# Loading FFN up-projection weights into the input projection's buffer during the prompt mixer

## The reference

```python
h = rmsnorm(x, g_mix) * (1.0 + scale_m) + shift_m
proj = h @ w_in                                   # 1024 -> 3072
q, k, v, g_ret, x_lru, g_lru = jnp.split(proj, offs, axis=-1)
o, s_ret_new = retention(rotary(q), rotary(k) * d ** -0.5, v, s_ret)
ret_out = silu(g_ret) * groupnorm(o)
xc, s_conv_lru_new = causal_dwconv(x_lru, s_conv_lru, conv_lru_w, conv_lru_b)
hl, s_h_new = rg_lru(xc, s_h, pos, w_r, b_r, w_i, b_i, lam)
lru_out = hl * gelu(g_lru)
x = x + gate_m * (jnp.concatenate([ret_out, lru_out], axis=-1) @ w_out)

h = rmsnorm(x, g_ffn) * (1.0 + scale_f) + shift_f
u = h @ w_up_conv                                 # 1024 -> 2816
gv = h @ w_up_gate                                # 1024 -> 2816
uc, s_conv_ffn_new = causal_dwconv(u, s_conv_ffn, conv_ffn_w, conv_ffn_b)
x = x + gate_f * ((gelu(uc) * gv) @ w_down)       # 2816 -> 1024
y = rmsnorm(x, g_final)
```

## Time and profile before

| | us |
|---|---|
| two timed runs | 1499.32 and 1509.76, median 1504.54 |
| the profiled execution | 1513.84 |
| its span on the slowest core, core 4 | 1512.2 |
| spans of the eight cores | 1488.4 to 1512.2 |
| mean granted TensorE clock of the cores | 0.822 to 0.835 of full speed |
| busy on core 4: PE, DVE, ACT, POOL | 985.5, 732.6, 416.2, 199.4 |

### The profile page before, as it was taken

The page is one execution under the profiler, slowest core; times in us unless marked ns, Lnnn a source line. Parts: engine busy times, 40 slices in busy tenths (PEclk is TensorE's granted clock), DMA queues, the critical chain, the costliest instruction groups (busy, mean ns, idle before and its releaser), DMA issues.

```text
span 1512.2 us, 15593 instructions; the slowest of 8 cores (1488.4 to 1512.2 us)
## 1 busy us (share of the span) xinstructions
PE 985.5 (65%) x4378; PEld 462.6 (31%) x4453; DVE 732.6 (48%) x1699; ACT 416.2 (28%) x702; POOL 199.4 (13%) x238
## 2 busy tenths in 40 slices
PE   1115517176677766777551799789878986998554
PEld 0002414133333333333221344334333333433222
DVE  0012045156677777777721364267426742674253
ACT  1000020235533424413302333233223323331011
POOL 1001000121211321311221200100010001000200
PEclk9557556588888999988785799899989998899877
DMA  9957523310101211100138993310031003000220
GB/s 154 173 92 115 112 71 102 125 42 15 42 1 42 84 42 42 57 28 28 57 119 173 180 171 61 124 43 1 1 125 43 1 0 126 15 1 26 87 43 8
DMA packets 46526, 104.85 MB, mean 69 GB/s; under 512 B 3428, under 2 KB 15169, under 8 KB 46393
## 3 DMA queue, kind: packets, MB, share of 16 engines
q0 software_dynamic: 18016, 38.54, 16.2%
q1 hardware_dynamic: 28041, 64.95, 13.5%
q10 hardware_dynamic: 384, 0.36, 0.1%
HBM read 120.29 MB, written 22.09 MB: 94 GB/s over the span
## 4 chain that ended last, share of the span: by engine, by line
PE 38%; DVE 20%; DMA 14%; issue 11%; ACT 8%; POOL 4%; another core or an unknown queue 3%; SPq 1%; DVEq 1%; POOLq 0%; ACTq 0%; PEldq 0%
PE ps L163 35%; DMA sb_wada<-w_ada 4%; DMA sb_wug_sb<-w_upg 3%; PE ps L166 3%; DVE sb_acc L187 3%; DMA sb_xa<-x_scr 3%; DVE sb_xc L187 2%; DVE sb_mq L179 2%; ACT sb_acc L176 1%; SPq L198 1%; DVE sb_ig L187 1%; DVE sb_xc L662 1%; DVE sb_hT L184 1%; DVE sb_yo L187 1%
## 5 line engine op out<-in xcount | busy, mean ns | idle before, releaser
L163 PE MATMUL ps<-sb_h2T,sb_wuc_sb 128*128 128x512 bf16 x688 | 173.0, 393 | 15.4 <-ACT sb_h2T L176 6.4
L163 PE MATMUL ps<-sb_wdn_sb,sb_aT 128*128 128x512 bf16 x692 | 166.0, 403 | 16.9 <-DVE sb_aT L179 14.2
L163 PE MATMUL ps<-sb_h2T,sb_wug_sb 128*128 128x512 bf16 x688 | 168.7, 385 | 3.0 <-DMA sb_wug_sb<-w_upg 2.1
L163 PE MATMUL ps<-sb_w_in_sb,sb_hT 128*128 128x512 bf16 x497 | 130.9, 413 | 35.6 <-DVE sb_mq L179 33.3
L187 DVE SCALAR_TENSOR_TENSOR sb_acc<-ps,sb_vfm,sb_acc 128x511 f32<-128x511 f32 (+1 forms) x176 | 131.5, 747 | 31.1 <-ACT sb_acc L176 22.0
L166 PE MATMUL ps<-sb_ident,sb_xn 128*128 128x128 f32 x256 | 46.1, 340 | 115.8 <-ACT sb_xn L176 80.2
L176 ACT ACTIVATE sb_acc<-sb_acc 128x512 f32<-128x512 f32 x88 | 55.4, 629 | 201.0 <-DVE sb_acc L187 162.5
L163 PEld LDWEIGHTS ps<-sb_wdn_sb,sb_aT 128*128 128x128 bf16 x704 | 72.4, 103 | 108.8 <-issue 37.0
L163 PE MATMUL ps<-sb_w_out_sb,sb_catT 128*128 128x512 bf16 x252 | 82.3, 493 | 30.0 <-DVE sb_xcar L192 24.0
L163 PEld LDWEIGHTS ps<-sb_h2T,sb_wuc_sb 128*128 128x128 bf16 x704 | 67.4, 100 | 112.8 <-issue 48.2
L163 PEld LDWEIGHTS ps<-sb_h2T,sb_wug_sb 128*128 128x128 bf16 x704 | 69.8, 99 | 89.0 <-issue 12.2
(11 more groups left out here) (226 smaller groups left out, 1337.9 us busy)
## 6 DMA issues: line engine op xcount, KB each, us to landing
sb_wada<-w_ada POOLq DMA_DIRECT2D x6, 2048.0 KB, 34.7
sb_xt<-xp SPq DMA_DIRECT2D x16, 512.0 KB, 3.7
sb_xr<-xp SPq DMA_DIRECT2D x16, 512.0 KB, 4.1
x_scr<-sb_x1t SPq DMA_DIRECT2D x16, 512.0 KB, 2.9
sb_xa<-x_scr SPq DMA_DIRECT2D x16, 512.0 KB, 4.3
sb_xb<-x_scr SPq DMA_DIRECT2D x16, 512.0 KB, 5.0
yp<-sb_yo SPq DMA_DIRECT2D x16, 512.0 KB, 3.0
sb_w_in_sb<-w_in POOLq DMA_DIRECT2D x8, 768.0 KB, 68.3
```

The source lines that it names most:

```text
L163: return self.S.add("pe", lambda e: e.matmul(out, lhsT, rhs, start=start, stop=stop), r, w)
```

## The change

- A buffer `arena` of [128, 24576] bf16 is allocated for the whole program. `w_in_sb` becomes a view of it; after the mixer three views of [128, 8, 1024] lie in it: `wuc` group 0, `wug` group 0 and `wuc` group 1. The remaining groups get buffers of their own in the FFN phase; the sum of memory is the same. `GroupedW` hides this from the code that reads the weights.
- At `tau` 16, after the `L2b` piece and ahead of `B2(14)`, `O(11)` and `B1b(15)`, `prefetch_ffn` issues six loads of 1 MB from POOL. Each lists as written its own keys and all eight `("w_in", kc)` keys.
- `wload` no longer issues those six loads: `wload[0]` is empty, `wload[1]` issues `wug` alone.

```diff
+        arena = sb("arena", [128, 8 * DPROJ], BF16)
...
+        def _aview(off):
+            return arena[:, off:off + 8192].rearrange("p (kc n) -> p kc n", kc=8)
+
+        wuc_g0, wug_g0, wuc_g1 = _aview(0), _aview(8192), _aview(16384)
...
+        WINK = [("w_in", kc) for kc in range(8)]
+
+        def prefetch_ffn():
+            for (dst, srcv, nm, gi, a, b) in ((wuc_g0, wuc_v, "wuc", 0, 0, 1024), (wug_g0, wug_v, "wug", 0, 0, 1024),
+                                             (wuc_g1, wuc_v, "wuc", 1, 1024, 2048)):
+                for h0 in (0, 4):
+                    k.dma(dst[:, h0:h0 + 4, :], srcv[:, h0:h0 + 4, a:b], (),
+                          [(nm, kc, gi) for kc in range(h0, h0 + 4)] + WINK, eng="pool")
...
-            w_in_sb = sbA("w_in_sb", [128, 8, DPROJ], BF16)
+            w_in_sb = arena[:, :].rearrange("p (kc n) -> p kc n", kc=8)
...
-            wuc_sb = sbB("wuc_sb", [128, 8, DFF], BF16)
-            wug_sb = sbB("wug_sb", [128, 8, DFF], BF16)
+            wuc_sb = GroupedW([wuc_g0, wuc_g1, sbB("wuc_g2", [128, 8, 768], BF16)])
+            wug_sb = GroupedW([wug_g0, sbB("wug_g1", [128, 8, 1024], BF16), sbB("wug_g2", [128, 8, 768], BF16)])
...
                     for h0 in (0, 4):
-                        k.dma(wuc_sb[:, h0:h0 + 4, a:b], wuc_v[:, h0:h0 + 4, a:b], (),
-                              [("wuc", kc, gi) for kc in range(h0, h0 + 4)], eng="pool")
-                        k.dma(wug_sb[:, h0:h0 + 4, a:b], wug_v[:, h0:h0 + 4, a:b], (),
-                              [("wug", kc, gi) for kc in range(h0, h0 + 4)], eng="pool")
+                        if gi >= 2 or not KPREF:
+                            k.dma(wuc_sb[:, slice(h0, h0 + 4), slice(a, b)], wuc_v[:, h0:h0 + 4, a:b], (),
+                                  [("wuc", kc, gi) for kc in range(h0, h0 + 4)], eng="pool")
+                        if gi >= 1 or not KPREF:
+                            k.dma(wug_sb[:, slice(h0, h0 + 4), slice(a, b)], wug_v[:, h0:h0 + 4, a:b], (),
+                                  [("wug", kc, gi) for kc in range(h0, h0 + 4)], eng="pool")
...
@@ -830,6 +863,8 @@
             Lpiece("L1", tau // 2)
         else:
             Lpiece("L2a", tau // 2)
+        if tau == NT:
+            prefetch_ffn()
         if tau == 4 * NST:
```

## The result

The changed kernel takes 1537.42 us (median of 11 runs, 1531.3 to 1572.3) beside 1505.86 us for the kernel before (median of 10 runs on the same chip). The ratio is 1.0208, with a 95% interval of 1.0179 to 1.0237: 31 us slower. The profiled execution took 1536.83 us, its span on the slowest core (now core 3) is 1535.3 us.

The account below looks back on a forecast made before the run. No engine was taken as full; a ring of waits held the mixer's end. 34.9 us delay + 2 tail - 4.5 FFN start = +32.4 us: 1546.2 us profiled, 1537 against the timed median; range 1519 to 1551.

Parts of the forecast that it names:

- The stall: Mixer's end: rs of tile 15 delayed on POOL behind six load issues that wait for each other, 34.9 us.
- d: One 1 MB weight load's time on POOL from issue to next issue, taken as 10.2 us.
- the cover: POOL's idle time before rs of tile 15, from 743.46 to 760.38, 16.9 us, which hides part of the waits.
- The middle of the two ends: Load time taken midway between 9.2 us (full queue) and 11.1 us (lone 2 MB loads), plus 0.1 for POOL's wake-up.
- The lone 2 MB rows: Profile rows of sixteen nearly lone 2 MB loads, 17.1 to 21.3 us, mean 19.0, used to bound d from above.
- the fast nor the slow loads of the rivals: Prefetch loads on POOL: fast, d 6.7 us, 1519 us, chance 0.12; slow, d 14.9 us, 1560 us, chance 0.11.
- the formula: Delay of rs of tile 15 on POOL: 5d + 0.8 - 16.9 us for six loads.
- The tail: Mixer's end from rs of tile 15 to the barrier: +2 us, as the sixth load is still in flight.
- The FFN's start: From barrier to up projection: -4.5 us, 2.5 from PE's waits for weights and 2 from earlier xa.
- 44.20 us of chain: Chain piece from 802.52 until the fourth up-projection megabyte lands at 846.72; its whole removal (1460 us) had chance 0.01.
- The line of 2%: Whole kernel: 30.1 us slower, about what a measurement can tell from no change, reached at d = 9.7.
- The rival "POOL is not held": POOL passes the six issues at once, no delay; net -4.5 to +11.5 us, 1500 to 1516 us, chance 0.04.

Follow-up runs that it names:

- first experiment: The changed kernel, but only the first of the six loads lists the w_in keys as written: 1.0109 of the kernel before.
- 2 MB kernel: The changed kernel with the same six megabytes as three chained loads of 2 MB: 1.0162 of the kernel before.
- four and six loads: Four: the changed kernel with only the four chained group 0 loads prefetched, 1.0101 of the kernel before. Six: the changed kernel itself, 1.0208.
- The last experiments: Kernel before with more xr and x1t buffers, gfin and gate row loaded after xa: 0.9922 of before; with two unchained loads prefetched too, 0.9881.
- The control on DVE: The kernel before, no prefetch, with rs of tile 15 on ACT and DVE and residual adds of tiles 11 to 15 on DVE: 0.9960 of before.

## Why the prediction was right, and where it was not

- **POOL waits for each load: right.** Five waits, named by the trace, and gone with the keys (first experiment). The stall was to be 34.9 us, it is 32.0: 2.3 less by d, 0.6 less by the cover.
- **d: right in size (9.74 measured from issue to issue, 10.2 taken), wrong in its parts.** Over the eight cores it is 9.33 to 10.39. I had split a load into 3.1 us fixed and 6.1 to 8.0 per MB; the 2 MB kernel shows about 1.7 and 8.1. Of the fixed part no row had shown the 0.4 at the end, and the 0.1 for POOL's wake-up was too small: on core 3 the first load lands after 10.85 us and the next issue comes at 11.40, 0.55 later, and so at the others. The middle of the two ends was near because a fixed part too large stood beside a rate too small. The lone 2 MB rows had the rate per MB right (8.0), and the full queue had it too low (6.1), but its sum of 9.2 came nearer than the other's 11.1, by the same two errors. That d came out within 0.5 us is in part luck, and five times d is most of the sum. Neither the fast nor the slow loads of the rivals came about. The estimate from the Trainium skill, "DMA: Bandwidth & Descriptors", section "Anatomy of one DMA", 6.8 us a load, is below every core here.
- **Cover of 16.9 us: right.** The first issue is at 742.89 (743.5 forecast), and four and six loads both fit the formula with it to 0.6 us.
- **The tail, +2 (0 to 4): measured +3.5.** In range; the sixth load was in flight beside the ring, as said (9.0 to 12.2 us from issue to landing). That this is the cause, and not PE's clock, no run shows by itself.
- **The FFN's start, -4.5: measured -3.4**, of which 2.7 are barrier to `xa`, 0.2 the way from there to `UP`, and 0.5 the first up projection. I had the two the other way round, 2.5 for the weights and 2 for `xa`. The point that mattered held: the 44.20 us of chain put down to `wug` was not there to be gained, since 28.3 us of norm and transpose run beside it. From the barrier to `UP` it is 35.8 us, not the 39 that I named as the sign, because I had started from core 4's 12.2 us to `xa` and not from the mean of 10.15. The last experiments show the other side: once `xa` comes 5 us earlier, the weights are waited for (+9.6 us), and only then does a prefetch shorten that stretch.
- **Sum: +32.4 forecast; +30.8 by the eight cores' mean, +31.6 by the medians.** Measured less forecast it is -2.9 in the stall, +1.5 in the tail, +1.1 at the FFN's start, and -1.4 in the stretches before and after, which I had at nothing: together -1.7. On core 4, slowest before, the stall and tail cost 35.7 + 2.7 us and 5.4 came back between the barrier and `UP`. The line of 2%, at which I had split my chances 0.53 to 0.46, lies inside the measured interval, so the runs favour neither side of it.
- **The rival "POOL is not held" was priced too low.** It didn't come about, but the first experiment makes it: I gave it -4.5 to +11.5 us, and the expectation on record 0 to +13; it measured +16. I had charged 5.2 us for each of three `xr` loads. One took 20.5 us (16 more than in the earlier trace rows), and the sum of bytes, not the single load, sets the price: 6 MB at 6 to 8 us are 37 to 49 us of the DMA engines, in a stretch of 55 us in which they were busy for a share of 0.31 already: 17 us. That is an estimate of 54 to 66 us of work for 55, too full to hide. This sum could have been made from the rows of before.

What stays open: that every further load costs 4 us and not the 6 to 8 that it takes. It would fit with idle DMA time that is left at the stretch's edges and in the ring's gaps, but no run parts these. The profiled executions of the kernels before and after also take 84.5 and 84.0 us from `UP` to `DOWN`, and all others without late weights 81 to 82. The control on DVE, whose FFN is the code of before, has 81.4: within the execution of before it is 81.3 on cores 0 and 1 and 87.6 on core 4. So it goes with the execution and not with an edit, and I can't attribute it. For the difference of the two it doesn't matter, since both have it.

## What to carry to other kernels

Before you prefetch on a compute engine's queue, list what each issue will wait for there and what stands behind it: six loads that "write" the same dead buffer wait for each other, and POOL's 1 us of `rs` came 32 us late. Then add up bytes: hidden is only what fits into the idle share of the DMA engines up to the next barrier, here two loads of six. And last ask what the consumer waits for at present; if it is not the weights, clear that first: only after it did the prefetch take time out of a stretch here (9.6 us of `UP` to `DOWN`).

## What was unexpected of the hardware

- Eight cores that load at once: a converting load of 1 MB (as bf16, 2 MB read) with no other weight load beside it took 7.9 to 11.6 us from issue to landing, mean 9.2 (loads 1 to 5 of the changed kernel), and with the next issue 9.74; one of 2 MB took 17.8 with it, so about 1.7 us + 8.1 per MB, slower per MB than in a full queue (6.1): single loads leave the DMA engines part idle (share 0.69 in the stall). What limits a single load no run shows.
- With that queue full (share near 1) transfers from the other queue stretch far beyond their own: a 0.5 MB load from 4.1 to 20.5 us, a 0.5 MB store from 2.8 to 10.5.
- Moving `rs` and the residual adds from POOL to DVE and ACT, made only as a control, gained 0.4% (0.9960, 0.9939 to 0.9981); five early `xr` loads and a second `x1t` gained 0.9%, since the ring of waits at the mixer's end had a load of 4 us and a store of 3 in each tile.
